# The first layer's modulation and projection, begun in quarters of the features

## The reference, cut

```
silu_c  = silu(c);  silu_cc = silu(c_ctx)
sh1, sc1, g1, sh2, sc2, g2 = split(silu_c @ ada_w[l] + ada_b[l], 6)      # the same with silu_cc
h  = rms_norm(x,  norm1_g[l]) * (1 + sc1)  + sh1
hc = rms_norm(xc, norm1_g[l]) * (1 + csc1) + csh1
qa, ka, va, qb, kb, vb = split(h @ w_in)                                 # the same with hc
```

## Time and profile before

| | |
|---|---|
| median of 3 runs | 1736.85 us (1736.84 to 1737.57) |
| profiled execution | 1737.95 us, its span 1736.1 us, mean granted clock of TensorE 0.998 |
| TensorE busy | 1703.8 us, 98% of the span |
| VectorE, ScalarE, GpSimd busy | 699.4, 387.0 and 201.9 us |
| moved by DMA | 499.32 MB, mean 288 GB/s |

### The profile page before, as it was taken

One profiled execution on the slowest core, in us unless ns is written; L12 is line 12 of the kernel. 1 busy time (PEld: TensorE's weight loads), 2 busy tenths in 40 slices (PEclk: granted clock), 3 DMA queues, 4 the chain that ended last, 5 costly groups with the idle time before them and its releaser, 6 DMA issues.

```text
span 1736.1 us, 30388 instructions
## 1 busy us (share of the span) xinstructions
PE 1703.8 (98%) x13210; PEld 1154.3 (66%) x13210; DVE 699.4 (40%) x1216; ACT 387.0 (22%) x777; POOL 201.9 (12%) x267
## 2 busy tenths in 40 slices
PE   7999989999999999999999999999999999999999
PEld 4777657888888888657665665656656566565664
DVE  4633686699956685362402003020130201202015
ACT  4422684432212224375100000000000000000010
POOL 2226231011101110542100000000000000000010
PEclk9999999999999999999999999999999999999999
DMA  9636301455586774133499999999999999999993
GB/s 358 217 135 215 110 2 50 145 194 182 173 288 228 277 249 169 49 134 128 166 416 405 408 423 410 420 419 412 423 410 421 416 414 424 409 419 418 409 421 141
DMA packets 134347, 499.32 MB, mean 288 GB/s; under 512 B 6704, under 2 KB 44592, under 8 KB 126032
## 3 DMA queue, kind: packets, MB, share of 16 engines
q1 hardware_dynamic: 130832, 491.60, 72.5%
q0 software_dynamic: 1920, 5.77, 1.0%
q10 hardware_dynamic: 1472, 0.11, 0.1%
HBM read 475.05 MB, written 22.41 MB: 287 GB/s over the span
## 4 chain that ended last, share of the span: by engine, by line
PE 91%; DVE 3%; ACT 2%; DMA 2%; POOL 1%; issue 1%; SPq 0%; POOLq 0%; DVEq 0%; ACTq 0%
PE ps L2506 33%; PE ps L2522 11%; PE ps L2317 7%; PE ps L2318 7%; PE ps L2319 7%; PE ps L2529 6%; PE ps L2163 2%; PE ps L2079 2%; PE ps L2149 2%; PE ps L2081 2%; PE ps L2080 2%; PE ps L2248 2%; PE ps L2193 2%; DMA ring<-in_ada_w 2%; PE ps L2217 1%; PE ps L2227 1%
## 5 line engine op out<-in xcount | busy, mean ns | idle before, releaser
L2506 PE MATMUL ps<-ring_up,xg 128*32 128x448 f32 x3840 | 370.1, 539 | 0.0
L2506 PEld LDWEIGHTS ps<-ring_up,xg 128*32 128x32 f32 x3840 | 227.2, 110 | 133.6
L1928 DVE TENSOR_TENSOR hid<-hid,ps 128x448 f32<-128x448 f32 x48 | 26.9, 617 | 525.5 <-PE ps L2506 525.5
L2506 PE MATMUL ps<-ring,xg 128*32 128x448 f32 x2304 | 225.8, 539 | 0.7 <-DVE xg L1894 0.7
L2506 PEld LDWEIGHTS ps<-ring,xg 128*32 128x32 f32 x2304 | 134.8, 110 | 83.1 <-issue 5.7
L2522 PE MATMUL ps<-ring_up,hidT 128*32 128x512 f32 x1024 | 128.1, 592 | 0.0
L2317 PE MATMUL ps<-hTh,fsa 128*128 128x512 f32 x328 | 127.7, 389 | 0.3 <-DVE hTl L1763 0.3
L2319 PE MATMUL ps<-hTl,fsa 128*128 128x512 f32 x328 | 127.6, 389 | 0.0
L1219 ACT ACTIVATE fsa<-ring 128x1024 fp32r<-128x1024 f32 (+2 forms) x73 | 68.8, 944 | 233.9 <-PE ps L2319 232.8
L1375 DVE SCALAR_TENSOR_TENSOR scr<-ring,scond,scr 128x512 f32<-128x512 f32 x140 | 120.2, 892 | 1.2
L1325 ACT ACTIVATE ytok<-ps 64x512 f32<-64x512 f32 x16 | 9.5, 592 | 406.1 <-PE ps L2529 406.0
(11 more groups left out here) (329 smaller groups left out, 2600.0 us busy)
## 6 DMA issues: line engine op xcount, KB each, us to landing
ring_up<-in_moe_w SPq DMA_DIRECT2D x80, 1792.0 KB, 10.8
ring<-in_moe_w SPq DMA_DIRECT2D x48, 1792.0 KB, 11.2
ring<-in_moe_w SPq DMA_DIRECT2D x24, 2048.0 KB, 14.4
ring_up<-in_moe_w SPq DMA_DIRECT2D x24, 2048.0 KB, 13.9
ring<-in_ada_w SPq DMA_DIRECT2D x23, 2048.0 KB, 8.0
ring_up<-in_moe_w SPq DMA_DIRECT2D x16, 1024.0 KB
ring<-in_ffn_w_gate SPq DMA_DIRECT2D x11, 1024.0 KB, 5.6
ring<-in_ffn_w_up SPq DMA_DIRECT2D x11, 1024.0 KB, 8.2
```

What stands on the lines that cost most here:

```text
L2506: ins = pe.matmul(ps[3 * z + t][32 * q:32 * q + 32, 0:FC], xg[:, k, 32 * t:32 * t + 32], w[:, c, FC * q:FC * (q + 1)], start=(k == 0), sto ...
```

## The change

The four chunks A0a become quarters of the features: chunk j holds the 256 shift and the 256 scale columns of k = 2j and 2j + 1, and comes in two loads. With each goes the row block of W0 0 for the same two k. All that follows goes by quarters: take, modulation (ScalarE now has the first latent tile of each quarter, GpSimd the three others), parts, and the projection of the first four units, in which the chunk j + 1 stands between the latents and the context of quarter j and its turn one step further on.

Besides, the order around it is changed. The first chunk is used after four of the context's sums; the root of the context, its reciprocal and the products stand behind the latents of quarter 0; ScalarE runs an unused root early, so that its table is loaded; one busy matmul is dropped; `gains` stands behind all low parts; the chunk A0b 0 goes behind the matmuls of x = 4, its transpose to x = 4 and its turn to x = 5. The scaled context tiles count on a semaphore of their own, `ctx_sc`, for which GpSimd waits. The diff, cut to its core:

```diff
 
-        ADA_BANK = (0, 1, 6, 5)
+        ADA_BANK = (5, 6, 5, 6)
         SC_BANK = (5, 4, 6, 7, 0, 1, 2, 3)
-        NORM0 = [(c, k) for h in range(2) for c in range(2) for k in range(4 * h, 4 * h + 4)]
+        NORM0 = [(c, k) for j in range(4) for c in range(2) for k in (2 * j, 2 * j + 1)]
         norm0_of = {ck: n + 1 for n, ck in enumerate(NORM0)}
-        pool0_of = {ck: n + 1 for n, ck in enumerate(ck for ck in NORM0 if ck not in ((0, 0), (0, 4)))}
+        pool0_of = {ck: n + 1 for n, ck in enumerate(ck for ck in NORM0 if ck[0] or ck[1] % 2)}
 
...
                 if (nm, j) == ("W1", 2):
                     load(g, rslot(g)[:, 0:KT * 160].rearrange("p (a b) -> p a b", b=160), cols(a["od_w_in"], 1024, 160))
-                elif (nm, j) == ("W0", 0):
-                    sp.dma_start(slot3(g, 512)[:, 0:2, :], cols(a["ev_w_in"][0:2 * P, :], 0, 512)).then_inc(s_w0, 16)
-                    sp.wait_ge(s_x[0], 16)
-                    sp.dma_start(slot3(g, 512)[:, 2:4, :], cols(a["ev_w_in"][2 * P:4 * P, :], 0, 512)).then_inc(s_x[0], 16)
-                elif nm in square:
-                    if (nm, j) == ("W0", 1):
-                        load(at["W0", 0], slot3(at["W0", 0], 512)[:, 4:KT, :], cols(a["ev_w_in"][4 * P:, :], 0, 512))
+                elif nm == "A0a":
+                    for half in range(2):
+                        load(g, slot3(g, 512)[:, :, 256 * half:256 * half + 256],
+                             cols(a["ada_w"][0], D * half + 256 * j, 256), wait=(half == 0))
+                    w0 = slot3(at["W0", 0], 512)[:, 2 * j:2 * j + 2, :]
+                    rows = cols(a["ev_w_in"][2 * j * P:(2 * j + 2) * P, :], 0, 512)
+                    if j in (1, 2):
+                        sp.wait_ge(s_x[j - 1], 16)
+                    sp.dma_start(w0, rows).then_inc((s_w0, s_x[0], s_x[1], slot_full[slot_of(at["W0", 0])])[j], 16)
+                    if j == 3:
                         sp.dma_start(vec[:, :], a["vec"].partition_broadcast(P)).then_inc(s_vec, 16)
                         sp.dma_start(cst[:, 0:CST_N - 32], a["cst"][:, 0:CST_N - 32]).then_inc(s_vec, 16)
+                elif (nm, j) == ("W0", 0):
+                    continue
+                elif nm in square:
                     w, c0 = square[nm]
-                    if (nm, j) == ("A0a", 1):
-                        sp.wait_ge(s_cond, 16)
-                        sp.dma_start(slot3(g, 512)[:, 0:4, :], cols(w[0:4 * P, :], 512 * A0A_COLS[1], 512)).then_inc(s_cond, 16)
-                        load(g, slot3(g, 512)[:, 4:KT, :], cols(w[4 * P:, :], 512 * A0A_COLS[1], 512))
-                        continue
-                    load(g, slot3(g, 512), cols(w, c0 + 512 * (A0A_COLS[j] if nm == "A0a" else j), 512))
...
 
             for c, k in NORM0:
-                    if (c, k % 4) == (0, 0):
+                    if (c, k) not in pool0_of:
                         continue
-                    if (c, k % 4) == (0, 1):
-                        pool.wait_ge(ada_rd, 2 if k == 1 else 4)
+                    if c == 0:
+                        pool.wait_ge(ada_rd, k + 1)
+                    else:
+                        pool.wait_ge(ctx_sc, k + 1)
                     tc = slice(c * S_LAT, (c + 1) * S_LAT)
                     pool.tensor_scalar(h0raw[:, k, tc], h0raw[:, k, tc], amod[:, 0, 0, k, c:c + 1], ada[:, 0, k, c:c + 1],
...
             act.wait_ge(eps_set, 1)
+            act.activation(rt8[:, 1, 0:1], eps[:, 0:1], ACT.Sqrt)
+
+            def token_root(c):
+                tc = slice(c * S_LAT, (c + 1) * S_LAT)
+                act.wait_ge(norm["n00"]["summed"], KT * c + KT)
+                act.activation(rt[:, tc], ps[6][:, tc], ACT.Sqrt, bias=eps[:, 0:1], scale=1.0 / D)\
+                   .then_inc(norm["n00"]["root"], 1)
+
             for c in range(2):
                 tc = slice(c * S_LAT, (c + 1) * S_LAT)
                 act.wait_ge(s_x[c], 16)
@@ -1150,16 +1160,15 @@
                     if k >= 4:
                         act.wait_ge(norm["n00"]["summed"], KT * c + k - 3)
                     act.activation(sq[k % 4][:, tc], xT[:, k, tc], ACT.Square).then_inc(norm["n00"]["square"], 1)
-                act.wait_ge(norm["n00"]["summed"], KT * c + KT)
-                act.activation(rt[:, tc], ps[6][:, tc], ACT.Sqrt, bias=eps[:, 0:1], scale=1.0 / D)\
-                   .then_inc(norm["n00"]["root"], 1)
+                if c == 0:
+                    token_root(0)
 
             def tokens_hi(c, k):
                 tc = slice(c * S_LAT, (c + 1) * S_LAT)
                 if (c, k) in pool0_of:
                     act.wait_ge(norm["n00"]["scaled"], pool0_of[c, k])
                 else:
-                    act.wait_ge(ada_rd, 2 if k == 0 else 4)
+                    act.wait_ge(ada_rd, k + 2)
                     ch.after(act.activation(h0raw[:, k, tc], h0raw[:, k, tc], ACT.Identity, bias=ada[:, 0, k, c:c + 1],
                                             scale=amod[:, 0, 0, k, c:c + 1]))
...
                     between(d)
 
-            for c in range(2):
+            def roots_inverted(c):
                 tc = slice(c * S_LAT, (c + 1) * S_LAT)
                 dve.wait_ge(norm["n00"]["root"], c + 1)
                 ch.after(dve.reciprocal(rstd[:, tc], rt[:, tc]))
-                for k in range(KT if c == 0 else 0):
-                    dve.tensor_tensor(h0raw[:, k, tc], xT[:, k, tc], rstd[:, tc], ALU.mult)
+
+            def latents_scaled(ks):
+                for k in ks:
+                    ins = dve.tensor_tensor(h0raw[:, k, 0:S_LAT], xT[:, k, 0:S_LAT], rstd[:, 0:S_LAT], ALU.mult)
+                return ins
 
             def context_scaled(ks):
                 tc = slice(S_LAT, 2 * S_LAT)
                 for k in ks:
-                    ins = dve.tensor_tensor(h0raw[:, k, tc], xT[:, k, tc], rstd[:, tc], ALU.mult)
-                return ins
+                    dve.tensor_tensor(h0raw[:, k, tc], xT[:, k, tc], rstd[:, tc], ALU.mult).then_inc(ctx_sc, 1)
...
-            context_scaled(range(3))
-            ada_first_blocks(1)
-            ch.after(context_scaled(range(3, 4)))
-
-            def ada_first_take(h):
-
-                dve.wait_ge(ada_tr, 2 * h + 2)
-                m = adam[:, 0:16, :].rearrange("p (w h m) c -> p h w m c", w=2, h=2)[:, h]
-                b = adabm[:, 0:16].rearrange("p (w h m) -> p h w m", w=2, h=2)[:, h]
-                dve.tensor_tensor(m, ps[7][:, 16 * h:16 * h + 16].rearrange("p (w m c) -> p w m c", w=2, c=2),
-                                  b.unsqueeze(3).to_broadcast([P, 2, 4, 2]), ALU.add).then_inc(ada_rd, 1)
-                dve.wait_ge(ada_rd, 2 * h + 1)
-                dve.scalar_tensor_tensor(out=amod[:, 0, 0, 4 * h:4 * h + 4, :], in0=ada[:, 0, 8 + 4 * h:12 + 4 * h, :],
-                                         scalar=1.0, in1=ng[:, 0, 0, 4 * h:4 * h + 4].unsqueeze(2).to_broadcast([P, 4, 2]),
+            def ada_first_take(j):
+
+                dve.wait_ge(ada_tr, j + 1)
+                m = adam[:, 0:16, :].rearrange("p (w j m) c -> p j w m c", w=2, j=4)[:, j]
+                b = adabm[:, 0:16].rearrange("p (w j m) -> p j w m", w=2, j=4)[:, j]
+                dve.tensor_tensor(m, ps[7][:, 8 * j:8 * j + 8].rearrange("p (w m c) -> p w m c", w=2, c=2),
+                                  b.unsqueeze(3).to_broadcast([P, 2, 2, 2]), ALU.add).then_inc(ada_rd, 1)
+                dve.wait_ge(ada_rd, 2 * j + 1)
+                dve.scalar_tensor_tensor(out=amod[:, 0, 0, 2 * j:2 * j + 2, :], in0=ada[:, 0, 8 + 2 * j:10 + 2 * j, :],
+                                         scalar=1.0, in1=ng[:, 0, 0, 2 * j:2 * j + 2].unsqueeze(2).to_broadcast([P, 2, 2]),
...
-                if (c, k) == (0, 4):
-                    ch.after(context_scaled(range(4, KT)))
-                    ada_first_blocks(2)
-                    ada_first_blocks(3)
-                if (c, k % 4) == (0, 0):
-                    ada_first_take(k // 4)
-                if c == 0 and k % 2 == 0:
-                    weights_lo(0, k // 2)
-                tokens_lo(c, k)
+                dve.tensor_reduce(lamt[:, 0:2], v3(dots[:, 0:128], 64), AX.X, ALU.add).then_inc(gain_rd, 1)
+
+            roots_inverted(0)
+            latents_scaled(range(4))
+            for j in range(4):
+                ada_first_blocks(j)
+                if j < 2:
+                    ch.after(latents_scaled(range(4 + 2 * j, 6 + 2 * j)))
+                ada_first_take(j)
+                weights_lo(0, j)
+                for k in (2 * j, 2 * j + 1):
+                    tokens_lo(0, k)
+                if j == 0:
+                    roots_inverted(1)
+                    context_scaled(range(4))
+                elif j == 1:
+                    context_scaled(range(4, KT))
+                for k in (2 * j, 2 * j + 1):
+                    tokens_lo(1, k)
+            gains()
 
             def between(x):
                 c = x // 4
-                if x % 4 == 3 and c < 6:
```

(35 more changed lines are left out.)

38 lines of the change are left out of this document (15 added, 23 removed).

## The result

| | kernel before | changed kernel |
|---|---|---|
| median | 1737.40 us (1736.84 to 1738.31, 6 runs) | 1746.33 us (1745.95 to 1747.77, 6 runs) |
| profiled execution, span | 1737.95, 1736.1 us | 1745.95, 1744.0 us |
| mean granted clock | 0.998 | 0.998 |

What follows compares the result with a forecast made beforehand. TensorE was taken as the bound, with a second bound in the chain behind unit 0. Delay 2.9 at x = 4, chunk 2.1 and clock 1.5 made 6.5 us; 1736.85 + 6.5 = 1743.4 us, range 1739.0 to 1748.5.

Steps and rivals of the forecast that it cites:

- What bounds it: Whole kernel: TensorE bounds it and waits little after 57 us, so a front delay or gain is handed on whole.
- Loads: DMA queue at the front: 1 KB rows cost 0.8 us a chunk; chunk 0 lands at 16.4 us, nothing runs dry.
- The early start: First projection matmul: starts at 21.7 us instead of 25.6, 3.9 us gained.
- The quarters: TensorE's first block: 27.7 us of work plus 3.5 us of waits, ending at 52.9 us instead of 53.87.
- Unit 0: First block's end: unit 0 finishes later, ScalarE squares at 49.7 us instead of 47.94, +1.75 us on the second bound.
- The gains: VectorE before unit 0's reduction: nine small operations now stand in the chain, +1.15 us.
- The chunk: A0b chunk moved from the wait at x = 2 to behind x = 4's matmuls: in the open, +2.1 us.
- The clock: TensorE around x = 4: long waits likely drop the granted clock to half, +1.5 us, bounds 0 and 3.
- the clock at the front (1): TensorE from about 14 to 16.4 us: clock falls there too, 2 to 3 us more, time 1745.9; chance 0.25.
- The skeleton (2): Front: no clock loss, 1 KB rows as fast as 2 KB, gains hidden; delay 3.05 us, time 1739.9; chance 0.2.
- The early start (3): First block: other engines deliver each quarter in time, so TensorE never idles there; time down to 1733.4 us; chance 0.04.
- A front set by the DMA queue (4): Front: DMA queue, not TensorE's order, sets it; block ends at 53.9 us, time 1742.9; counted within the forecast's 0.51.

Runs made afterwards that it cites:

- the late unit's run: First experiment: kernel before, with the last eight steps of TensorE's first block alternating latents and context as in the change; 1742.80 us, ratio 1.0027.
- the kernel before with the short distance: Tenth experiment: kernel before, with unit 1's scaling moved ahead of the two low weight pieces on VectorE; 1736.92 us, ratio 0.9998.
- the narrow rows' run: Second experiment: kernel before, with each A0a chunk loaded in two loads of 256 columns (1 KB rows); 1740.92 us, ratio 1.0017.
- The last run: Twelfth experiment: changed kernel, quarters kept, gains ahead of chunk 3's transpose, A0b 0 at x = 2, unit 1's scaling ahead of the weight pieces; 1740.54 us.
- that of the chunk back: Third experiment: changed kernel, with chunk A0b 0, its transpose and its turn back at x = 2, 3 and 4; 1743.04 us, ratio 1.0030.
- eighth: Changed kernel with the block's second half in the old order, gains before the last low parts and A0b 0 at x = 2; 1740.50 us, ratio 1.0013.
- eleventh: Changed kernel with old second half, early gains, A0b 0 at x = 2, and unit 1's scaling ahead of the low weight pieces; 1739.25 us, ratio 1.0012.
- four runs with the cut chain: Ninth to twelfth experiments, unit 1's scaling ahead of VectorE's low weight pieces, in the kernel before or versions of the changed one; 1744.65, 1736.92, 1739.25, 1740.54 us.

## Why the prediction was right and wrong

The direction and the mechanism were right: the early start does not reach the end of the block, unit 0's late end sets the wait, the chunk is in the open, the clock falls where it was said to. The size was 1.4 us too small against the traces' 7.9 us, and 2.4 against the medians. That it came so near is in part luck: inside the block, waits put 1.9 us too high stood against work put 3.1 us too low, and 1.5 us came back through a half clock that only some executions of before have. Point by point:

- *What bounds it.* A delay at the front is handed on: right, but not whole. Of 9.4 us at the last A0b chunk 7.9 are left. "Nothing behind gives it back" failed: the half clock of the earlier trace rows, 1.5 us, is no fixed cost behind the front. It is absent in the changed kernel, in the late unit's run and in the kernel before with the short distance; from 195 to 200 us the clock is at 0.66 in the narrow rows' run and in the last, and at 0.72 in that of the chunk back. In the changed kernel TensorE comes to that place with the same wait ahead of its turn, 1.57 us at 199.78; what decides it there stays open.
- *Loads.* Chunk 0 at 16.4: used at 16.23, and the later ones were never waited for. Right, and the second experiment measured the row size in the kernel before.
- *The early start.* 3.9 us predicted, 3.1 found. The step took the distance from a chunk's end to the first projection from before, 3.5 us; here the rest of the context's sums (18.09, 1.99 us) stands between the chunk and its turn at 20.01.
- *The quarters.* The end of the block was put at 52.9 and is 54.9. The start is 0.8 of that. The waits inside were over-estimated: 1.6 us (four waits for VectorE's low parts), not 3.5. The work was under-estimated, 54.9 - 22.5 - 1.6 = 30.8 us, not 27.7. One cycle shows it: from 31.79, where the latents of one quarter begin, to 40.49 it is 8.70 us, less 24 x 0.228 = 5.47 for matmuls and 0.43 idle leaves 2.80 for the chunk and the turn, where I had put 1.72 + 0.25 = 1.97. The rows say where: 1.85 us from the chunk to the next matmul, and a step of three matmuls takes 0.82 instead of 0.69 after each change and 0.78 before it. Three such cycles are 2.5 us of the 3.1; of the rest, 0.3 lies in the first quarter and 0.3 in the last. This is the term that failed most.
- *Unit 0.* The step "on which all turns" held in kind: +1.75 predicted, +3.6 measured (51.56 against 47.94), since the block ends later. From the square to the end of the block it is 3.4 us (54.93 - 51.56), where I had put 3.2 (52.9 - 49.7), so the whole of this miss is the block's. The late unit's run gives the order alone: 3.1 us, two steps (2.7) and a chunk 3 used 0.4 later (35.48 against 35.11).
- *The gains.* +1.15 predicted; 0.9 measured, by the distance from square to reduction (1.5 us, and 0.6 with the gains early).
- *Unit 1's turn.* 60.05 predicted, 61.61 measured; from the reduction on it is the distance of before, 8.5 us. x = 4: +2.9 predicted, +4.8 measured. This one term holds the miss: 1.9 us.
- *The chunk.* +2.1 predicted; 1.7 at x = 5 and 0.4 more at the next chunk. Right.
- *The third weight chunk.* Cost 0, bounds 0 and 2: 0.8. It was issued at 72.57, not at 68.6, and took 14.3 us, so ScalarE had it at 86.86, not at 82.
- *The clock.* +1.5 predicted; in the trace 1.7 in the matmuls of x = 4 (62.38 to 69.65, 7.3 us, where it is 5.6 in before), and 0.4 more in the turn ahead of them, which stands in the 4.8. Taken away alone it gives 2.1 there.
- *Sum.* Predicted 2.9 + 2.1 + 0 + 1.5 = 6.5; measured 4.8 + 2.1 + 0.8 + 1.7 - 1.5 = 7.9. The -1.5 stands only against an execution of before with its half clock; the median from which the forecast started, 1736.85, is most likely one without.

The rivals: the clock at the front (1) did not fall, TensorE was busy for 3.76 of the 4.00 us from 14 to 18 and stayed at 1.00; the sums ran nearly until the chunk came. The skeleton (2) is out by every term. The early start (3) came to nothing even in the eighth and eleventh runs, with the old second half. A front set by the DMA queue (4) is excluded by the single wait of 0.20 us.

The last run is 1.9 us behind the eleventh at the gate mark where the turn explains 1.65: at the last A0b chunk it is still 1.64 (183.63 against 181.99), and the other 0.25 comes at the place of the half clock, which the eleventh has not. Open is what makes the clock fall near 192 and 768 us in some executions and not in others.

## What to carry to other kernels

Where a block of work feeds a chain behind it, ask when each member of the block ends, not when the block begins: finer interleaving makes the first work earlier and the first result later. Each piece of other work set into a dense stretch of matmuls costs more than its own duration (here 0.8 us a quarter more than reckoned for a chunk and a turn), and work that fills a wait is free only as long as it stays there. Before two engines are put side by side to shorten a chain, read what each takes alone and beside the other. And before a difference of one or two microseconds between two traces is read as the edit's, compare the granted clock all along both: here one stretch of half clock, there or not, goes with up to 1.7 us.

## What the runs showed of the hardware

- VectorE and GpSimd slow each other. In all four runs with the cut chain the gain took 2.28 to 2.31 us (1.26 to 1.30 away from the pieces) and the two weight pieces 3.43 to 3.45 (2.36 away from the gain). One after the other they would take 1.26 + 2.36 = 3.6 us, so side by side gives next to nothing. The Trainium skill ("GPSIMD Engine Reference", Specifications) says that GpSimd shares its SBUF interfaces with VectorE and contends with instructions that have two SBUF inputs. The weight pieces have two, and the rows agree.
- The clock does not follow from the length of a wait alone. Behind a turn, a chunk and then a wait of some 2.5 us it was 0.66 from 60 to 65 us in the first run (2.51), 0.67 in the eighth (2.49) and 1.00 in the third (2.52). Which of the differences between these runs decides was not tried.
- Changing between the projection's matmuls (fp32r weights and tokens) and those of a chunk or a turn (f32) comes with a longer step of three on either side, 0.78 ahead and 0.82 behind instead of 0.69, as the rows from 33.98 to 39.21 of the changed kernel show. The 0.82 behind is not tied to the change of kind: after a plain wait of 0.43 us between two projection matmuls the first step takes 0.81 too (40.49 to 41.30). What causes the 0.78 ahead was not tried.
